# Loads, stores and vector work moved within the recurrence heads of a hybrid HGRN2 / short-convolution trunk

## What is computed

```python
for l in range(2):
    mod = silu(c) @ ada_w[l] + ada_b[l]            # shift, scale, gate; twice
    h = modulate(rmsnorm(x), sh1, sc1)
    if l == 0: y = hgrn2_mixer(h, hc, ...)         # both directions, 8 heads of 128
    else:      y = short_conv_mixer(h, ...)
    x = x + g1 * rmsnorm(y)
    x = x + g2 * rmsnorm(swiglu(modulate(rmsnorm(x), sh2, sc2)))
```

```python
S_t = diag(f_t) @ S_(t-1) + outer(k_t, v_t)        # 128 x 128 state
o_t = S_t.T @ q_t
```

## Time and profile before

| what | value |
|---|---|
| profiled execution | 2715.53 us |
| its span, first to last instruction | 2713.8 us |
| around the span | 1.7 us |
| PE busy | 2619.1 us, 97% |
| DVE busy | 1661.2 us, 61% |
| ACT busy | 965.9 us, 36% |
| POOL busy | 1145.1 us, 42% |
| DMA | 269.07 MB, 99 GB/s on average |
| heads 1 to 6 | about 170 to 716 us, 90 to 92 us a head |
| head 7 | 716 to 768 us, then `fill` |

### The profile page before, as it was taken

The page is one execution under the profiler, slowest core; times in us unless marked ns, Lnnn a source line. Parts: engine busy times, 40 slices in busy tenths (PEclk is TensorE's granted clock), DMA queues, the critical chain, the costliest instruction groups (busy, mean ns, idle before and its releaser), DMA issues.

```text
span 2713.8 us, 36296 instructions
## 1 busy us (share of the span) xinstructions
PE 2619.1 (97%) x12848; PEld 2187.1 (81%) x12848; DVE 1661.2 (61%) x2376; ACT 965.9 (36%) x1856; POOL 1145.1 (42%) x788
## 2 busy tenths in 40 slices
PE   7999999999989799999999989999999999999998
PEld 6888888888878578888888877888787888888886
DVE  5378767877863765665655565666447555555556
ACT  5344443444333742222233254111254322223233
POOL 2112332343220146555666632444305665556662
PEclk8999999999989899999999999999999999999999
DMA  6222441333170332211112132333413111111113
GB/s 250 78 93 94 171 164 66 113 141 132 54 270 17 117 139 78 81 67 62 62 62 85 47 145 88 120 113 112 190 52 135 50 68 54 46 46 51 57 47 147
DMA packets 76132, 269.07 MB, mean 99 GB/s; under 512 B 8688, under 2 KB 8688, under 8 KB 72944
## 3 DMA queue, kind: packets, MB, share of 16 engines
q1 hardware_dynamic: 76016, 267.53, 27.2%
HBM read 217.16 MB, written 50.33 MB: 99 GB/s over the span
## 4 chain that ended last, share of the span: by engine, by line
PE 87%; DVE 6%; ACT 2%; POOL 2%; issue 1%; DMA 1%; SPq 0%; DVEq 0%; POOLq 0%; ACTq 0%
PE psum L1196 19%; PE psum L1197 18%; PE psum L1198 18%; PE psum L1727 5%; PE psum L1729 5%; PE psum L1728 5%; PE psum L1393 2%; PE psum L1438 2%; PE psum L1440 2%; PE psum L1439 2%; PE psum L1380 1%; PE psum L1407 1%; PE psum L1363 1%; PE psum L1253 1%; DVE c_set L2421 1%
## 5 line engine op out<-in xcount | busy, mean ns | idle before, releaser
L1196 PE MATMUL psum<-x_hi,unit 128*128 128x512 f32 x1232 | 484.1, 393 | 5.8 <-DVE x_lo L2421 5.4
L1197 PE MATMUL psum<-x_lo,unit 128*128 128x512 f32 x1232 | 481.2, 391 | 0.0
L1198 PE MATMUL psum<-x_hi,unit 128*128 128x512 f32 x1232 | 480.8, 390 | 0.0
L2421 DVE TENSOR_TENSOR c_set<-c_set,psum 128x512 f32<-128x512 f32 x352 | 233.7, 685 | 352.8 <-PE psum L1198 187.4
L1113 POOL TENSOR_TENSOR unit_sum<-ffn_raw 128x512 f32<-128x512 f32 x200 | 268.5, 1343 | 388.6 <-PE psum L1196 227.8
L2421 DVE TENSOR_TENSOR y<-y,psum 128x512 f32<-128x512 f32 x288 | 193.8, 686 | 159.1 <-PE psum L1729 154.8
L1196 PEld LDWEIGHTS psum<-x_hi,unit 128*128 128x128 f32 x1232 | 232.3, 189 | 61.3 <-ACT c_set L1841 6.2
L1118 POOL TENSOR_TENSOR unit<-unit_sum,unit 128x512 fp32r<-128x512 f32 x200 | 258.0, 1298 | 55.8 <-ACT unit L1841 55.6
L1198 PEld LDWEIGHTS psum<-x_hi,unit 128*128 128x128 f32 x1232 | 232.3, 189 | 48.8
L1197 PEld LDWEIGHTS psum<-x_lo,unit 128*128 128x128 f32 x1232 | 232.3, 189 | 47.3
L1196 PE MATMUL psum<-h_hi,w_hi 128*128 128x512 f32 x624 | 262.7, 421 | 0.2 <-DVE h_lo L2421 0.2
(11 more groups left out here) (303 smaller groups left out, 5238.5 us busy)
## 6 DMA issues: line engine op xcount, KB each, us to landing
ffn_raw<-in_w_ffn_in SPq DMA_DIRECT2D x80, 512.0 KB, 3.5
ffn_raw<-in_w_ffn_out SPq DMA_DIRECT2D x44, 512.0 KB, 4.1
w_raw<-in_w_hgrn_in SPq DMA_DIRECT2D x40, 512.0 KB, 3.5
ada_raw<-in_ada SPq DMA_DIRECT2D x32, 512.0 KB, 4.8
conv_ada_raw<-in_ada SPq DMA_DIRECT2D x32, 512.0 KB, 4.4
units_kept<-stage_unit SPq DMA_DIRECT2D x28, 512.0 KB, 2.7
unit<-units_kept SPq DMA_DIRECT2D x28, 512.0 KB, 5.0
rows_kept<-stage_row SPq DMA_DIRECT2D x12, 1024.0 KB, 4.0
```

What stands on the lines that cost most here:

```text
L1196: begin = pe.matmul(out_ap, hi[:, a:b], rhs_hi, start=first, stop=False)
L1197: pe.matmul(out_ap, hi[:, a:b], rhs_lo, start=False, stop=False)
L1198: return begin, pe.matmul(out_ap, lo[:, a:b], rhs_hi, start=False, stop=last)
L2421: V.tensor_tensor(dst, a, b, op).then_inc(S[sem], 1)
```

## The change

The diff changes orders only; no instruction is added, removed or resized.

1. SP: ada panels 2 and 3 of head h are issued behind panel (h,4), ahead of panel (h+1,0), no longer behind panel (h+1,1). Ada 0 and 1 stand directly behind stores B, and stores C behind panel (h,2). After head 7 the loads of rows 0 to 2 stand ahead of stores B, no longer behind them.
2. ACT: the high parts of spot B stand ahead of the three BWD `k_tok` copies, no longer behind them.
3. DVE: the gate product and ada 0 and 1 stand ahead of the FWD states, no longer behind them.

```diff
--- before.py
+++ after.py
@@ -37,6 +37,7 @@
 G_CONV = G_FFN + 4
 FFN_HIDDEN_PANELS, FFN_OUT_PANELS = 4, 2
 
+HEAD_ADA = ((), (0, 1), (), (), (2, 3))
 CONV_ADA = ((0, 1), (2,), (3,))
 
 
@@ -757,10 +758,6 @@
                 else:
                     stage_panels(phase)
 
-            def head_ada(h, first):
-                for a in (first, first + 1):
-                    ada_panel(h * ADA_GROUP + a, a % 2)
-
             def head_loads(h, parity):
                 n = N_HEADS + h * HEAD_PANELS
                 for i in range(HEAD_PANELS):
@@ -770,17 +767,14 @@
                         stage_stores(h - 1, A_SPOT)
                     elif i == 1:
                         stage_rows(h - 1, C_SPOT)
-                        if h > 1:
-                            head_ada(h - 1, 2)
                         stage_stores(h - 1, B_SPOT)
+                    elif i == 2 and h > 0:
                         stage_stores(h - 1, C_SPOT)
-                        head_ada(h, 0)
-                    elif i == 2 and h > 0:
                         if h == 1:
                             sp.wait_ge(S["turned"], T0[1])
                         stage_begin(h)
-                    elif i == 4 and h == 0:
-                        head_ada(h, 2)
+                    for a in HEAD_ADA[i]:
+                        ada_panel(h * ADA_GROUP + a, a % 2)
 
             for h in range(HEADS):
                 head_loads(h, h % 2)
@@ -824,14 +818,13 @@
                              ).then_inc(S[f"unit_loaded{k % 4}"], 16)
 
             stage_stores(HEADS - 1, A_SPOT)
-            head_ada(HEADS - 1, 2)
-            stage_stores(HEADS - 1, B_SPOT)
             sp.wait_ge(S["gemm_full"], O_CONV - 2)
             sp.wait_ge(S["ctx_full"], 3 * HEADS)
             for slot in range(3):
                 sp.wait_ge(S[f"stage_stored{slot}"], max(unit_stored(p, j) for p in range(3) for j in range(slot, PRODUCTS, 3)))
             for r in range(3):
                 row_load(r)
+            stage_stores(HEADS - 1, B_SPOT)
             stage_stores(HEADS - 1, C_SPOT)
             sp.wait_ge(S["ada_step"], 8 * HEADS)
             row_load(3)
@@ -2181,10 +2174,9 @@
                         act.wait_ge(S["scan_full"], hs * SCAN_USES + (SCAN_USES + U_LEVEL))
                         evacuate(3, 0, cols(v_t, 0, CTX))
                         panel_high(4)
+                        stage_highs(hg, B_SPOT)
                     for part in range(3):
                         key_tokens(BWD, part)
-                    if hg is not None:
-                        stage_highs(hg, B_SPOT)
                     if hg is None:
                         for i in (7, 8, 9):
                             part_out(i)
@@ -2793,16 +2785,12 @@
                     for i in FAR_LEVELS:
                         decay_level(i)
                     if hg is not None:
-                        for part in range(3):
-                            states(FWD, part)
                         gate_product()
                         for a in range(2):
                             ada_rows(hg, a)
-                    else:
+                    for d in (FWD, BWD):
                         for part in range(3):
-                            states(FWD, part)
-                    for part in range(3):
-                        states(BWD, part)
+                            states(d, part)
                     if hg is not None:
                         for a in range(2, ADA_GROUP):
                             ada_rows(hg, a)
```

## The result

The changed kernel takes 2746.9 us (median of 4 runs, 2746.6 to 2750.2) against 2715.0 beside it: ratio 1.0117, 95% interval 1.0100 to 1.0136. It is slower, as forecast, but by 32 us where 19 were forecast; 2734.7 was the forecast and 2746 the end of its range. The profiled execution took 2749.15 us, span 2747.4.

The account below looks back on a forecast made before the run. PE, busy 97% of the span, was taken as the bound, so only its waits count. 11.1 + 3.6 + 6.0 - 1.5 + 0 = +19.2 us on 2715.53 gave 2734.7 us, range 2716 to 2746.

Parts of the forecast that it names:

- The sign and the places of the loss: Whole kernel: slower by 19.2 us, with PE waiting for states in heads 1 to 3 and k_tok in heads 4 to 6.
- Row heads: Heads 1 to 3: states late by 3.7 us each, +11.1 us, plus half clock behind the stalls, +3.6 us.
- POOL gets two turns: Rival: heads 2 and 3 lose 5.9 us each, with more half clock; +29 us, 2744 in all; chance 0.18.
- One turn: Heads 1 to 3: DVE's ada steps alternate with POOL's operations, `w_lo` only behind step 3; states 3.7 us late per head.
- The sequence of low part, step, low part, step: Head 3: POOL and DVE alternate, low part 1 to 369.5, step 1 to 369.8, low part 2 to 372.0, step 2 to 372.5.
- Pair heads: Heads 4 to 6: late stores A delay the `k_tok` copies, +6.0 us; the wait in head 5 goes, -1.5 us.
- The first unit: Heads 4 to 6: behind the late ada and panel loads, the first unit store lands at 654.5.
- Half clock: Heads 1 to 3: PE at 1.2 GHz behind the new stalls, 1.2 us each, bounds 0 and 3; +3.6 us.
- just under 3.2 us: Heads 1 to 3: new stalls of some 3.1 us, just under the 3.2 us stall that had half clock around it.
- The end: Head 7 and behind: later `o_tok` against a shorter wait for the mix, 0 us, bounds -6 and +4.
- The queue order: Head 7: mix and unit stores of spot B wait behind 3 MB of row loads, landing at 761.7 against 757.7.
- The 1.5 us in head 5: Head 5: PE's wait for `o_tok` goes because part 2 starts POOL's chain earlier, -1.5 us.

Follow-up runs that it names:

- part 3 alone: Kernel before with only the gate product and ada steps 1 and 2 moved ahead of the FWD states on DVE: 2731.0 us.
- With the stores on time: Changed kernel with the fourth ada panel of a head loaded behind panel (h+1,0) and the stores A: 2739.2 us.
- after without the early row loads: Changed kernel with the stores of spot B of head 7 ahead of the row loads again: 2743.2 us.
- part 1 alone: Kernel before with only SP's new order in the heads, the loads behind head 7 as before: 2784.4 us.
- the early row loads alone: Kernel before with only the stores of spot B of head 7 put behind the row loads: 2720.1 us.
- parts 2 and 3 without part 1: Kernel before with the ACT and DVE parts, SP and POOL as before: 2724.2 us.
- part 2 alone: Kernel before with only ACT's high parts of spot B ahead of the BWD k_tok copies: 2724.8 us.

## Why the prediction was wrong

The sign and the places of the loss were right; three terms of the sum were too small, by 5.8 + 9.0 + 1.4 us; less the 1.7 us of the start, that is about the 14.4 us by which the profiled execution missed the sum.

- **Row heads: 14.7 forecast, 20.5 measured, +5.8.** The step that failed is "POOL gets two turns", put at 0.18 and described as a matter of 0.1 us. It happened in heads 2 and 3. One turn was priced right: the states started 3.7 us late by forecast, and part 3 alone costs 14.6 us in heads 1 to 3 for 14.7. The second turns add 4.1 us of waits (13.4 for 9.3), and the half clock is longer too. The sequence of low part, step, low part, step was right to 0.3 us. The Trainium skill (SBUF — State Buffer, "Who interferes with whom") says that the order of issue decides who blocks. The runs agree only with an offset to the records: DVE's always started first, and it won when it was ahead by 0.050 us or more and lost at 0.044 or less. Nothing in the kernel before told this in advance. A forecast should have given both orders like chances, as the price of one is 3.7 and of the other 5.9; afterwards it was 7 heads of 10 with the second turn.
- **Pair heads: 4.5 forecast (6.0 - 1.5), 13.5 measured, +9.0.** Seen from PE's first product, stores A leave 6.4 us later (forecast 6.8), and the sums wait for them:
```profile
676.36 1.75 SPq L751 DMA_DIRECT2D units_kept<-stage_unit  x3
```
```profile
683.01 2.51 POOL L1051 TENSOR_TENSOR stage_unit_sum<-stage_up_gate 128x512 f32<-128x512 f32 x2 [5.26 <-DMA units_kept<-stage_unit]
```
```profile
686.72 0.48 PE L1356 MATMUL psum<-ident,k_all 128*128 128x128 f32 x1 [2.81 <-ACT k_tok L1834]
```
The first unit lands 1.0 us later than worked out, so the wait is 2.8 to 3.3 us and not 1.6: 9.1 + 0.8 us of waits where 6.0 were forecast, 3.9 more. The other 5.1 are half clock, 3.4 us behind each of these waits, for which the sum had nothing. The mechanism itself is shown: with the stores on time the heads cost 3.3 us.
- **Half clock, which is part of both: 3.6 forecast (3 × 1.2), 13.6 measured.** Wait plus half of the stretch at half clock gives each head: 3.2 + 3.4, 5.1 + 1.7, 5.1 + 3.4, 3.3 + 1.7, 2.9 + 1.7 - 1.5, 2.8 + 1.7 = 34.5 us, against 34.0 by the landmarks. The forecast took "just under 3.2 us" for mostly safe. In heads 1 to 6 of these runs stalls of 1.2 to 1.9 us were followed by none, and those of 2.3 to 5.1 us by 3.4 or 6.8 us, with one exception: in head 1 of "after without the early row loads" the clock stayed full behind 3.2 us. The same wait of 3.2 us in head 1 had 6.8 us of half clock in the first execution of the changed kernel, 3.4 in the second and none there, and the head cost 6.0, 4.7 and 3.8 us. (With part 1 alone, waits of some 7 to 12 us had 6.8 to 20.5 us around them.)
- **The end: 0 forecast, +1.4 measured here and +4.5 with the early row loads alone.** The queue order was right: 12.2 and 13.1 us behind the rows, not 5. The section of the Trainium skill that was weighed against it (DMA: Bandwidth & Descriptors, "Two DMAs through the same engine are not ordered") is about when data can be relied on, and says too that descriptors of one queue start in order; it gives no time. But 9.8 us had been taken over from two stores that stood behind less. In the changed kernel the row loads, which answer to the earlier trace rows, leave only 9.2 us behind head 7's first product, where 10.3 were forecast (748.1) and 16.7 were before:
```profile
779.30 1.27 SPq L810 DMA_DIRECT2D hgrn_row<-rows_kept  x3
```
```profile
units_kept<-stage_unit SPq DMA_DIRECT2D x2, 512.0 KB, 12.2
```
That 1.4 is near the forecast's 0 is luck: parts 2 and 3 without part 1 gain 7.0 us from head 7 to the end, for which the forecast had nothing, and part 1 costs 8.4 us there, where the forecast's upper bound was 4. How the 8.4 divide between the row loads (4.2 us by the landmarks where they stand alone) and the rest of part 1 was not told apart.
- **Parts 1 and 2 as gains.** The 1.5 us in head 5 went, as forecast. That part 2 alone costs 9 us, because it brings POOL beside DVE's steps, was not foreseen, nor that part 3 removes this.

## What to carry to other kernels

An idle gap on DVE is room for such steps only if POOL is idle there too: the same four steps took 2.7 us alone and 11.2 beside POOL. Lay out both timelines before filling it. When a load is moved ahead of stores on one queue, follow the stored buffers to the end of the chain, since the first consumer is not the dearest (69 us, where the first consumer would have given 5). Parts that each lose can win together and the reverse, so test combinations. And where a new stall of PE is as long as those of 2.3 us and more here, add half of the stretch at half clock that followed them, 1.7 or 3.4 us.

## What was not expected of the hardware

- Two operations whose records start within 0.06 us of each other on DVE and POOL go in either order, in the same program: 2.94 us against 0.75 us for the same DVE instruction. A start 0.050 us or more ahead won for DVE in all five cases, one of 0.044 or less lost in all 16.
- DVE instructions with an input in PSUM ran at full speed beside POOL (3.2 us for eight states in every kernel), while those with two inputs in SBUF took 6.15 us for 2.4. Step 1, whose inputs are one large SBUF tile and a scalar column, was held up as well: 2.61 us for 0.48.
- Unit stores behind 3 MB of loads and 1 MB of mix stores in one queue took 13.1 us where 5.1 was usual.
